# One projection eviction and one attention stage rewritten: q and k stored in two parts, columns by residue, and TensorE's order turns, values, scores

## The reference, cut to what matters

```python
for window, dil in ((128, 1), (512, 4), (2048, 16)):       # three branches, 8 heads of 64
    # positions regrouped by residue mod dil, blocks of 128 queries,
    # keys: the previous block of the same residue and the current one
    s = jnp.einsum('brcqhd,brckhd->brchqk', qb, kw) * (Dh ** -0.5)
    s = jnp.where(valid, s + bias, NEG_INF)
    m = jnp.max(s, axis=-1, keepdims=True)
    e = jnp.exp(s - m); den = jnp.sum(e, axis=-1)
    o = jnp.einsum('brchqk,brckhd->brcqhd', e, vw) / den
    lse = m + jnp.log(den)
wts = jax.nn.softmax(jnp.stack(lses), axis=0)              # the branches are mixed by their denominators
```

## Time and profile before

| | us |
|---|---|
| median of 3 runs (lowest, highest) | 3026.03 (3024.14, 3026.6) |
| the profiled execution: its time | 3026.8 |
| its span | 3025.2 |
| PE busy in the span | 2773.8 (92%) |
| DVE busy | 1393.4 (46%) |
| ACT busy | 1285.8 (43%) |
| POOL busy | 373.3 (12%) |

### The profile page before, as it was taken

The page is one execution under the profiler, slowest core; times in us unless marked ns, Lnnn a source line. Parts: engine busy times, 40 slices in busy tenths (PEclk is TensorE's granted clock), DMA queues, the critical chain, the costliest instruction groups (busy, mean ns, idle before and its releaser), DMA issues. The chain is left out here.

```text
span 3025.2 us, 39394 instructions
## 1 busy us (share of the span) xinstructions
PE 2773.8 (92%) x14411; PEld 2392.2 (79%) x14411; DVE 1393.4 (46%) x2755; ACT 1285.8 (43%) x2521; POOL 373.3 (12%) x255
## 2 busy tenths in 40 slices
PE   6999996999956399599999999999999999997998
PEld 5999996999945388478888888888888888785886
DVE  1110424655667677344444445554444444544333
ACT  3333324655631576333333344443333333444554
POOL 2434332331100122000000000000000000000000
PEclk9999997999977699799999999999999999998999
DMA  4545437543131445422222246752222235762221
GB/s 160 191 162 167 129 119 192 144 110 94 42 122 22 147 157 167 126 60 67 80 67 80 94 170 210 258 173 66 81 66 78 67 132 207 244 216 96 78 78 44
DMA packets 308027, 375.41 MB, mean 124 GB/s; under 512 B 21393, under 2 KB 221393, under 8 KB 305786
## 3 DMA queue, kind: packets, MB, share of 16 engines
q1 hardware_dynamic: 293962, 324.82, 34.5%
q0 software_dynamic: 13888, 48.25, 4.1%
HBM read 290.20 MB, written 86.94 MB: 125 GB/s over the span
## 5 line engine op out<-in xcount | busy, mean ns | idle before, releaser
L2041 PE MATMUL ffn_bank<-ffn_hi,ffn_w_hi 128*128 128x512 f32 x1408 | 548.5, 390 | 0.0
L2042 PE MATMUL ffn_bank<-ffn_lo,ffn_w_hi 128*128 128x512 f32 x1408 | 548.2, 389 | 0.0
L2043 PE MATMUL ffn_bank<-ffn_hi,ffn_w_lo 128*128 128x512 f32 x1408 | 548.2, 389 | 0.0
L1949 DVE SCALAR_TENSOR_TENSOR ffn_conv<-tail_shared,ffn_taps,ffn_conv 128x512 f32<-128x512 f32 x176 | 132.1, 750 | 419.6 <-ACT ffn_conv L1868 419.6
L2041 PEld LDWEIGHTS ffn_bank<-ffn_hi,ffn_w_hi 128*128 128x128 f32 x1408 | 264.7, 188 | 55.1
L2043 PEld LDWEIGHTS ffn_bank<-ffn_hi,ffn_w_lo 128*128 128x128 f32 x1408 | 264.6, 188 | 55.0
L2042 PEld LDWEIGHTS ffn_bank<-ffn_lo,ffn_w_hi 128*128 128x128 f32 x1408 | 264.7, 188 | 54.8
L1866 ACT COPY tail_shared<-ffn_bank 128x512 f32<-128x512 f32 x176 | 103.3, 587 | 454.6 <-PE ffn_bank L2043 451.8
L1932 DVE TENSOR_TENSOR ffn_w_lo<-ffn_w,ffn_w_hi 128x2048 fp32r<-128x2048 f32 x92 | 210.8, 2292 | 168.3 <-ACT ffn_w_hi L1845 168.3
L2060 PE MATMUL ffn_bank<-ffn_w_hi,ffn_a_hi 128*128 128x512 f32 x704 | 275.6, 391 | 2.6 <-DVE ffn_a_lo L1936 2.6
L2061 PE MATMUL ffn_bank<-ffn_w_lo,ffn_a_hi 128*128 128x512 f32 x704 | 274.6, 390 | 0.0
(11 more groups left out here) (294 smaller groups left out, 5404.5 us busy)
## 6 DMA issues: line engine op xcount, KB each, us to landing
ffn_w<-in_ffn_w_up SPq DMA_DIRECT2D x88, 512.0 KB, 5.2
ffn_a<-ffn_act SPq DMA_DIRECT2D x176, 256.0 KB, 5.7
ffn_w<-in_ffn_w_down SPq DMA_DIRECT2D x40, 1024.0 KB, 7.1
in_w<-in_w_in SPq DMA_DIRECT2D x36, 1024.0 KB, 6.2
ffn_act<-tail_shared POOLq DMA_DIRECT2D x88, 256.0 KB, 2.7
mixed_part<-branch_results SPq DMA_DIRECT2D x16, 792.0 KB, 5.4
z_rows<-in_result SPq DMA_DIRECT2D x80, 128.0 KB, 2.0
branch_results<-att_part SPq DMA_DIRECT2D x8, 1056.0 KB, 6.0
```

Source lines behind the costliest of these rows:

```text
L2041: pe.matmul(out[:, :], w_hi[w][:, n, k, :], hi[:, k, cols], start=(k == 0), stop=False)
L2042: pe.matmul(out[:, :], w_hi[w][:, n, k, :], lo[:, k, cols], start=False, stop=False)
L2043: mm = pe.matmul(out[:, :], w_lo[w][:, n, k, :], hi[:, k, cols], start=False, stop=(k == KC - 1))
```

## The change

- **Projection.** For a q or k unit ACT copies the bank twice, once rounded (`result_hi`) and once as it is; POOL subtracts the two (`result_lo`); SP stores both parts, to `qk_hi` and `qk_lo`. On POOL the split of the next block's weights is put ahead of the results of this one.
- **Attention.** No splitting any more: SP loads six finished pieces of a head (q high over q low, k high twice, k low twice). For branches 1 and 2 POOL copies q, k high and k low into buffers whose columns lie by residue, six copies a head, so that `score` reads neighbouring columns. Values have a column pair of ones beside them: 66 columns, whose product also gives the sum of the exps; the exp on ACT no longer sums. Results of a pair stand as least, sum, values, values, sum, least. The loop over four heads is gone: all 160 units are written out, waits are on constants, and the `sem_inc` instructions that stood before DVE's maxima and POOL's splits are gone. Values are buffered once, by branch; biases come ahead of them.
- **Order on PE.** A step is now turn(n-3), weigh(n-4), score(n). DVE's and ACT's order stay.
- **Mixers.** The same instructions on the new layout.

```diff
-            with pe.Fori(0, steps) as i:
-                for n in range(U + RING + 1):
-                    if n < U:
-                        score(i, n)
-                    if 0 <= n - RING < U:
-                        turn(i, n - RING)
-                    if 0 <= n - RING - 1 < U:
-                        weigh(i, n - RING - 1)
+            for n in range(U + RING + 1):
+                if 0 <= n - RING < U:
+                    turn(n - RING)
+                if 0 <= n - RING - 1 < U:
+                    weigh(n - RING - 1)
+                if n < U:
+                    score(n)
...
-                    out, q = score_bank[n % 3][:, at:at + width], query_columns(q_parts[j % 2], b, first + m)
-                    pe.matmul(out, q, key_columns(k_hi[j % 2], b, first + m, prev, blocks), start=True, stop=False)
-                    mm = pe.matmul(out, q, key_columns(k_lo[j % 2], b, first + m, prev, blocks), start=False, stop=True)
+                    out = score_bank[n % 3][:, at:at + width]
+                    col = column_of(b, blk)
+                    queries = q[:, col:col + P]
...
+                    pe.matmul(out, queries, keys(k_hi), start=True, stop=False)
+                    mm = pe.matmul(out, queries, keys(k_lo), start=False, stop=True)
...
+            for j in range(HEADS):
+                pool.wait_ge(head_loaded[j % 2], (j // 2 + 1) * 6 * DMA)
+                for b in range(1, NB):
+                    dil = BRANCHES[b][1]
+                    if j:
+                        pool.wait_ge(scored, (j - 1) * UH + branch_end[b])
+                    for n in (1, 2, 0):
+                        nc.gpsimd.tensor_copy(spread[b - 1][n].rearrange("p (r c) -> p r c", r=dil),
+                                              near[j % 2][n].rearrange("p (c r) -> p r c", r=dil)).then_inc(spread_ready, 1)
...
-                dve.wait_ge(scored, i * U + (n + 1))
-                dve.wait_ge(exp_ready, i * UB + (blocks_to[n - RING + 1] if n >= RING else 0))
-                dve.sem_inc(st.dve_passed, 1)
+                dve.wait_ge(scored, n + 1)
+                if n >= RING:
+                    dve.wait_ge(exp_ready, blocks_to[n - RING + 1])
...
+            load_head(0)
+            load_bias(0)
+            for b in range(NB):
+                load_vals(0, b)
+            load_head(1)
...
-                nc.scalar.copy(result[:, u % RING, 0:width], product_bank[u % RING][:, 0:width]).then_inc(copied, 1)
+                if is_qk[u]:
+                    nc.scalar.copy(result_hi[:, r, :], product_bank[r][:, :]).then_inc(result_hi_ready, 1)
+                nc.scalar.copy(result[:, r, 0:width], product_bank[r][:, 0:width]).then_inc(copied, 1)
...
+            split_w(0)
+            for g, b, B in blocks():
+                if B + 1 < G * NBLK:
+                    split_w(B + 1)
+                for u in units_of(B):
+                    if is_qk[u]:
+                        split_result(u)
```

More of the change, by code:

```diff
@@ L232, in attention_units, with column_of @@
     return units
-def query_columns(qT, branch, block):
+def column_of(branch, block):
     dil = BRANCHES[branch][1]
     chunk, residue = divmod(block, dil)
[L239 to L254, removed]
@@ L257, in attention @@
-def attention(nc, qk, v, bands, bands_stored, partial, ident):
-    T = qk.shape[2]
-    PAIRS = qk.shape[0] // 2
+    return residue * (BRANCHES[2][0] // dil) + chunk * P
+def attention(nc, qk_hi, qk_lo, v, bands, bands_stored, partial, ident):
+    T = qk_hi.shape[2]
+    PAIRS = qk_hi.shape[0] // 2
     NB = len(BRANCHES)
     BL = T // P
[L269 to L273, removed]
-    blocks_to = [0]
[L275 to L292, removed]
-    with Stage(nc, "att") as st:
[L295 to L301, removed]
@@ L322, in _, with place, operands @@
+        def place(n):
+            j, i = divmod(n, UH)
+            return (j,) + units[i]
+        def operands(j, b):
+            return near[j % 2] if b == 0 else spread[b - 1]
         @block.sync
         def _(sp):
[L324 to L327, removed]
@@ L347, in store @@
[L347 to L361, removed]
@@ L363, in step @@
[L363 to L383, removed]
+            def load_head(j):
+                pair, rows = j // 2, slice(j % 2 * HEAD, (j % 2 + 1) * HEAD)
+                if j >= 2:
+                    sp.wait_ge(scored, (j - 2) * UH + branch_end[0])
+                    sp.wait_ge(spread_ready, (j - 1) * (NB - 1) * PARTS)
+                q, k_hi, k_lo = (t.bitcast(F32) for t in near[j % 2])
+                for dst, src in ((q[0:HEAD, :], qk_hi[pair][rows, :]), (q[HEAD:P, :], qk_lo[pair][rows, :]),
+                                 (k_hi[0:HEAD, :], qk_hi[PAIRS + pair][rows, :]), (k_hi[HEAD:P, :], qk_hi[PAIRS + pair][rows, :]),
+                                 (k_lo[0:HEAD, :], qk_lo[PAIRS + pair][rows, :]), (k_lo[HEAD:P, :], qk_lo[PAIRS + pair][rows, :])):
+                    sp.dma_start(dst, src).then_inc(head_loaded[j % 2], DMA)
@@ new lines, in exponential, with copy_summed @@
+                                         ACT.Exp, bias=part[:, b, first + m, LEAST[h]:LEAST[h] + 1], scale=-1.0).then_inc(exp_ready, 1)
+            def copy_summed(n):
+                j, b, first, count, prev = place(n)
+                h = j % 2
+                act.wait_ge(summed, n + 1)
+                nc.scalar.copy(part[:, b, first:first + count, 1 + h * ROW - h:ROW + h * ROW - h],
+                               sum_bank[n % 2][:, 0:count * ROW].rearrange("p (n d) -> p n d", d=ROW)[:, :, 1 - h:ROW - h]).then_inc(summed_copied, 1)
@@ L543 @@
+            for n in range(U + RING + 1):
+                if n < U:
+                    exponential(n)
+                if 0 <= n - RING - 1 < U:
+                    copy_summed(n - RING - 1)
 class Chain:
@@ L757, in units_of, with stores_through @@
             return range(units_to[B], units_to[B + 1])
+        is_qk = [columns[B % NBLK] < QK for B in range(G * NBLK) for _ in units_of(B)]
+        qk_to = [0]
+        for u in range(U):
+            qk_to.append(qk_to[-1] + is_qk[u])
+        def stores_through(u):
+            return sum(2 if is_qk[v] else 1 for v in range(u % RING, u + 1, RING)) * DMA
         @block.sync
@@ L1258, in mix_and_project @@
         g = st.sb("gain", [P, KC])
-        part = [st.sb(f"part{r}", [P, NB, heads, ROW]) for r in range(RING)]
+        part = [st.sb(f"part{r}", [P, NB * heads // 2, PAIR]) for r in range(RING)]
         rows = [st.sb(f"rows{r}", [P, D]) for r in range(RING)]
```

334 lines of the change are left out of this document (186 added, 148 removed).

## The result

The changed kernel takes 3301.86 us (median of 4 runs, 3288.41 to 3318.02); the kernel before took 3025.09 beside it (4 runs, 3022.92 to 3026.6). The ratio is 1.0918, 95% interval 1.0864 to 1.0971: slower by 9%. The prediction had the sign and the ring that makes the kernel slower, but kept the clock high, and missed the time: 3178 was forecast, and the range ended at 3290. The runs of the changed kernel also lie further apart (0.9%) than those of the kernel before (0.1%).

The account below looks back on a forecast made before the run. PE's issue was taken to bound both stages before; after, a PE-DVE ring in attention. 3026.8 - 4.5 + 3 + (520 - 367.4) = 3178 us, chance 0.68; range 3148 to 3290.

Parts of the forecast that it names:

- the ring: Attention: last score, DVE's maxima, DVE's copy, PE's value products, next score run in series each unit; stage 520 us.
- Its size: Attention unit: 3.24 us with four score matmuls, including handover 0.16 (ends 0.05 and 0.28); four-block unit 3.90.
- The clock: Attention: PE stays at the high clock level in all units, since none of its pauses exceeds 1.3 us.
- the rival: Attention: the clock falls too, 1.0 to 1.35 us more a unit; 3346 if all low, 3262 if half; chance 0.22.
- the +3 us for the start: Attention's start: PE enters at the low clock level, three units at 1 us more each.
- The rule cited in the prediction: Attention: frequent brief PE pauses make the clock swing between its levels, which would put the time near 3262.
- The start: Attention's start: PE begins as before at 476.4, biases land earlier at 480.1; -4.5 us, bounds -8 and 0.
- The projection: Projection: extra ACT copies, POOL subtractions and stores fit in idle time; cost 0, or 19 us if ACT lost cover.
- POOL's copies: Attention: 48 rearranging copies, 1.96 to 4.6 us each, cost 0; uncovered only beyond 10.8 us a copy.
- Packed columns, exp without sum, 66 columns: Attention: branches 1 and 2 issue scores like branch 0, gain mostly lost in waiting; exp 0, wider value products 0.
- the third rival: Attention: PE stays the bound, DVE's leg is covered and packed columns alone count; 2951 us, chance 0.03.
- The marks: Attention profile signs: value products wait over 150 us, DVE waits some 290 for scores, PE busy some 60%.

Follow-up runs that it names:

- kernel 1: The changed kernel with PE's old order of a step (scores, turns, value products), everything else of the change kept: 2952.85 us, ratio 0.9760.
- kernel 2: The changed kernel, PE's new order kept, with DVE copying the turned unit before taking the new maxima: 2974.78 us, ratio 0.9825.
- kernel 5: The changed kernel with four idle transposes of the identity per unit, between turns and value products on PE: 3152.52 us, ratio 1.0419.
- kernel 6: The changed kernel with two idle transposes of the identity per unit, between turns and value products on PE: 3157.97 us, ratio 1.0436.
- kernel 9: The changed kernel with PE's old order; for q and k, DVE subtracts from PSUM, without ACT's second copy or POOL's subtraction: 2963.39 us, ratio 0.9793.
- kernel 8: The changed kernel with PE's old order and without POOL's copies by residue, so scores read strided columns: 3034.86 us, ratio 1.0029.
- kernel 3: The kernel before the change with only PE's order of a step changed, to turns, value products, scores: 3392.83 us, ratio 1.1214.

## Why the prediction failed, step by step

- **The ring: right.** Between a score and the value product stands DVE's whole leg; kernels 1 and 2 each open the ring and get 349 and 327 us back.
- **Its size: right within 6%.** 3.24 was forecast and 3.10 measured at the same clock. Nearly all of the difference is the handover: 0.04 (848.90 to 848.94), the lower of my ends, where I took 0.16. Four-block units were put at 3.90; in kernel 5 they take 3.68 (586.21 to 589.89). Kernels 5 and 6, in which the clock holds, come to 3152.5 and 3158.0, under the 3178 by 20 to 26. The stage was to take 523 us from the first maximum and took some 500 in kernel 6 (the 502 less 2 from PE's first score to the first maximum).
- **The clock: the step that failed.** The sum took every unit at the high level, and gave 0.22 to the rival. The argument against it was that the pauses of the earlier trace rows came in few pieces and none of the ring's is over 1.3 us: it took for granted that only long pauses lower the clock (in the trace of before the 2.85 us are one pause, 930.49 to 933.34). The longest waits of the value products were 1.4 us, and yet the clock fell at the start of five heads, and was 0.50 from 560 to 700. The second half of the error is the +3 us for the start, three units at the low level: it took for granted that the clock rises in the ring, and it stayed low for 16 units, until about 540. Both together cost the difference to kernel 5, 3301.86 - 3152.52 = 149 us. The rival's price for a two-block unit was right: 1.0 to 1.35 us were forecast, and 4.40 - 3.10 = 1.30 measured. But its total took the low end (168 / 160 = 1.05), and a four-block unit costs 5.30 - 3.68 = 1.62, so that its 3346 for all units was too low; that the time lies between 3346 and the 3262 for half of them is partly luck. Of the 277 us that the change lost, the forecast's sum held 151. The range stopped at two thirds of the units at the low level, and it was about 130 of the 160.
- **The rule cited in the prediction.** The changed kernel's clock goes between 0.50 and 1.00 from stretch to stretch. The Trainium skill ("TensorE: Matmul & The Clock Gate", section "A second HAM failure mode: psum-queue depth-cycling") says that short frequent pauses of PE make its clock swing between the two levels. The trace agrees in that it swings, with five rises and five falls after the start; but the regular pauses themselves ran at 1.00 from 844 to 882, and the low level took five sixths of the stage, not the half that I read into the rule.
- **The start: half right.** 4.5 us were to be gained and 1.6 were (first maximum at 482.95 after 484.56). The biases came no longer behind the values, but PE's first operands came at 481.14 and not at 476.4, because the projection ended later. Kernel 1 gained 2.5 (482.08).
- **The projection: wrong by 4.8 us.** Its last matmul is at 460.79. Cost 0 was argued from ACT's idle 280 us. 3.9 of the 4.8 us are three waits of PE for the next rows; that ACT's longer list pushes these back fits kernel 9 but is not shown. 19 us, the end for an uncovered ACT, were far from it.
- **POOL's copies: mis-sized, without effect.** They take 3.8 us, twice the row that I took as nearest (which is recorded as a COPY, and these as CASTs), and inside my far end of 4.6; 48 of them are 177 to 182 us of a stage of at least 286, and in kernel 1 PE still waits for none.
- **Packed columns, exp without sum, 66 columns: right.** Branches 1 and 2 are spaced like branch 0 (0.12), PE in kernel 1 takes 1.81 and 2.24 a unit against the 1.81 and 2.30 of the working, and the third rival's 2951 was the time of the change without its order (2952.85).
- **The marks.** The wait of the value products was to be over 150 us and is 103; DVE's wait some 290 and is 419; PE's busy share 60% and is 83%. The low clock bends all three the same way: in kernel 6, mostly at the high level, they are 117, 269 and 75%, with the transposes counted as busy and lying in the first of the waits. The 60% was too low even so: at the high level the changed kernel has 70% (840 to 880).

## What to carry to other kernels

When an edit brings a short pause into each step of a loop, price it twice: at the present clock, and at the low one with every matmul stretched. Then ask two things of the clock and not one: what could lower it (here the start of a head), and whether a pause is left in each step at the low level, as it was here, where the clock stayed low for up to 156 us. If both answers are bad, the low price belongs in the sum and not among the rivals. Where two in-order queues feed each other, look for the operation on the other engine that stands behind a wait for what this one issues last: either queue can open the ring. Where a pause can't be removed, filling part of it with idle matmuls can give the clock back; removing it gives more (2952.9 against 3152.5).

## What the runs showed of the hardware

- A loop can stay at the low level for long. There the regular unit of the changed kernel pauses 0.62 of 4.40 us, and the clock was 0.50 for 156 us on end (560 to 716). The same units, pausing 1.04 of 3.10 us, ran at 1.00 from 848 to 867. So one order of work was seen at either level for many units.
- Two transposes of the identity a unit (0.38 us at the high level) were enough to bring the clock back in about 6 us after a fall, where PE's pauses had shrunk to 0.26 and 0. The granted clock in 560 to 700 went from 0.50 to 1.00. From four to eight nothing more is gained (3152.5, 3152.8). What the chip goes by, these runs don't tell.
- One pause of 3.12 us between units that have none (kernel 8) was followed by a granted clock of 0.53 from 684 to 709.
- A handover of scores from PE to DVE took 0.28 us in the kernel with the loop, and again in kernel 3, which has the loop and the new order (600.64 + 0.42 to 601.34); it took 0.04 in the one that is written out with constants in its waits. Whether the register values or the missing semaphore instruction make the difference was not tried.
- POOL's CAST of 128x2048 to fp32r took 3.88 us where it reads with a stride of 4 and 3.68 with 16, against the 1.96 of the regrouping COPY. What of this is the stride and what the cast was not tried.
